# Two score steps of a pair moved together in the step order of both attentions

## The chip, the cores and the metric

The kernel runs on one core of a Trainium2 chip. The metric is the device time of one execution in microseconds (us), the median of several runs. TensorE does matrix products, ScalarE and VectorE work on their results, GpSimd does little here, SyncE issues the loads. Each engine runs its own instructions in program order and waits on semaphores for the others. TensorE writes its products into PSUM, eight banks of 128 x 512 float32 each.

## The reference

A model of three mixers: a first block of two layers over 528 positions (16 learned ones and 512 tokens) and a second block. The first layer's mixer has two attentions side by side, and only these are touched by the change. Both are causal softmax attentions with 8 heads each:

```
s = einsum(q, k) * scale            # plus F[t] - F[s] in the forgetting attention
s = where(mask, s, NEG)
p = softmax(s)
o = einsum(p, v)                    # 64 values a head
```

The forgetting attention has heads of 64 with RMS-normed queries and keys. The latent attention (MLA) has 64 plain and 32 rotated dimensions a head; its queries, keys and values are projected from normed latents of 384 and 256 columns, which makes work between and beside the attentions. After both come the output projection, an MLP, a layer with a short convolution, another MLP and the second block.

## The kernel before

All of float32 matrix work is done with operands split in a high and a low part, three products for one. The eight attention pairs are numbered c = 0 to 7, with two heads in each: c = 0 to 3 are the forgetting attention, c = 4 to 7 the latent one. Pairs are pipelined: while pair c is being finished, the scores of pair c + 1 are prepared. `fox_ring` (L143) writes TensorE's order out as a list of steps, which `fox_pe` runs one after the other:

- `("s", c, i)`, called plain step si here (L739): scores with queries down and keys along, in four query blocks i of 128. They are used for the row maximum alone, which VectorE takes (L924). s3 is 512 keys wide, s2 400, s1 272, s0 256.
- `sm` : the same for the 16 learned positions (maximum at L931, combined at L934).
- `nt`, the turn (L830): VectorE's negated maxima are transposed; VectorE then writes them as rows (L941, L942, "shift").
- `("u", c, j)`, called turned step uj here (L756): scores with keys down and queries along, shifted by the maxima. ScalarE takes their exponentials into `prob` (L872): 128x1024 for u0, 128x832 for u1 (with 16x32 at L871), 128x544 for u2, 128x288 for u3.
- `pm` (L846) and `pv` (L859): the products of probabilities with values, 4 and 20 matrix products. `pv` has banks of its own.
- `lat` (pairs 1 and 2, L1106): sums of squares of the latents. ScalarE makes a scale of them (L1032, L1033), VectorE multiplies the latents by it (L1039). `bq` and `bk` (pairs 4 and 5, L1096): an inverse norm broadcast for the queries and keys of pair c + 2; VectorE multiplies by it (L1188 and L1189 for bq, L1195 and L1196 for bk), ScalarE and VectorE then split the results (L1174 to L1182, L1200 to L1207).

All steps but `pv` and `sum` share three buffers of two PSUM banks each, dealt out in turn: step n takes buffer n % 3. `fox_take` (L688) makes a step wait until the buffer's last user, the step three places before it in the list, has been read:

```
older = [x for x, n in fox_nth.items() if n < fox_nth[step] and fox_slot[x] == fox_slot[step]]
reader = {"s": "max", "sm": "meta_max", "nt": "shift", "u": "exp", "pm": "meta_out"}[kind]
pe.wait_ge(fx[reader], fox_count(*older[-1]))
```

The order of ScalarE and VectorE is written by hand as well, in `fox_act` (L863) and `fox_dve` (L926). ScalarE runs for each pair: exponential of u0, conversion of pair c - 1's output (L889), exponential of u1, then in pair 1

```
latent_scale_act(act, 0)
mla_weights_act(act, 0)
```

(L903, L904: the scale, then conversions of a weight matrix, L1058 and L1060) and in pair 2 the same with another matrix (L1063), then the exponentials of u2 and u3 and, after `pv`, the inverse of the sums (L883 to L886). In pairs 4 and 5 the splitting of a query follows the exponential of u2 and that of a key the one of u3. VectorE runs for each pair: the output (L949, L950), the maximum of s3, the remainder of the output (L954), in pairs 1 and 2 the latent products, in pairs 4 and 5 the products of bq; then the maximum of s2, in pairs 4 and 5 the products of bk; the maximum of s1; in pairs 1 and 2 the remainder of the weights (L1069, L1074), in pairs 4 and 5 that of the rotated query (L1200, L1201); the maximum of s0; the meta maximum; the shift.

Of the kernel before, what the change touches and what calls it, by code (L numbers as in the profile page):

```python
# [142 lines left out]
def fox_ring():  # L143

    out = [("sm", 0), ("s", 1, 3), ("nt", 0), ("s", 1, 2), ("u", 0, 0), ("s", 1, 1), ("u", 0, 1), ("s", 1, 0), ("u", 0, 2), ("sm", 1),
           ("u", 0, 3), ("pm", 0), ("nt", 1), ("pv", 0)]
    for c in range(1, 4):
        body = [("u", c, 0), ("s", c + 1, 3), ("u", c, 1), ("lat", c - 1), ("s", c + 1, 2), ("u", c, 2), ("s", c + 1, 1), ("u", c, 3),
                ("s", c + 1, 0), ("sm", c + 1), ("pm", c), ("nt", c + 1), ("pv", c)]
        out += [x for x in body if x[1] < (2 if x[0] == "lat" else 4)]  # L150
    out += [("pq", 0), ("pq", 1), ("sum", 0), ("pq", 2), ("sum", 1), ("pq", 3), ("sum", 2), ("pr", 0), ("sum", 3), ("pr", 1), ("sum", 4), ("rot", 0),
            ("pr", 2), ("sum", 5), ("rot", 1), ("pr", 3), ("sum", 6), ("rot", 2), ("pk", 0), ("sum", 7), ("rot", 3), ("pk", 1),
            ("sum", 8), ("pk", 2), ("sum", 9), ("pk", 3), ("sum", 10), ("kr", 0), ("kr", 1), ("sum", 11), ("sum", 12), ("bq", 4), ("v", 0),
            ("bk", 4), ("v", 1), ("v", 2), ("bq", 5), ("s", 4, 3), ("s", 4, 2), ("bk", 5), ("s", 4, 1), ("s", 4, 0), ("sm", 4), ("nt", 4)]
    for c in range(4, 8):
        body = [("u", c, 0), ("s", c + 1, 3), ("u", c, 1), ("bq", c + 2), ("s", c + 1, 2), ("u", c, 2), ("bk", c + 2), ("s", c + 1, 1), ("u", c, 3),
                ("s", c + 1, 0), ("sm", c + 1), ("pm", c), ("nt", c + 1), ("pv", c)]
        out += [x for x in body if x[1] < 8]
    return out
# [13 lines left out]
def program(nc, io, out):  # L173

    ctx = ExitStack()
    with ctx:
# [490 lines left out]
        fx = sems("fox", "squares sums full scales normed q_hi q_lo max meta_max shift exp meta_out pv inv o_done out_hi out_lo")  # L667
        fox_first = [[("s", 0, 3), ("s", 0, 2)], [("s", 0, 1), ("s", 0, 0)], []]
        fox_order = fox_ring()
        fox_slot, fox_nth = {}, {}  # L670
        for n, step in enumerate(sum(fox_first, [])):
# [1942 lines left out]
```

## Time and profile before

| | |
|---|---|
| median of 3 runs | 1817.6 us (1816.02 to 1818.84) |
| the profiled execution | 1817.29 us, span 1815.5 us |
| granted TensorE clock, mean of the span | 0.967 |
| TensorE (PE) busy | 1743.3 us, 96% |
| VectorE (DVE) busy | 885.2 us, 49% |
| ScalarE (ACT) busy | 633.8 us, 35% |
| first attention (pairs 0 to 3) | from about 143 to 221.5 us |
| second attention (pairs 4 to 7) | from 285.4 to 364.5 us |

### The profile page before, as it was taken

The page shows a single profiled execution, that of the slowest core. Times are in us where ns is not written, and L with a number is a line of the kernel's source. Part 1 is how long each engine was busy: PE and PEld are TensorE (multiplying, and loading weights), DVE is VectorE, ACT ScalarE, POOL GpSimd, SP SyncE. Part 2 cuts the span into 40 slices and gives each one's busy share as a digit, 9 for nine tenths or more (in the row PEclk, how much of TensorE's full clock was granted, in tenths as well). Part 3 has the DMA queues.
Part 4 walks back from the last instruction along what each step waited for, and adds up shares of the span by engine and source line. Part 5 has one row for each costly group of instructions (what it writes and reads, how often), then busy time and mean ns, then how long its engine had stood idle before and what let it go on. Part 6 is the DMA issues. An engine that isn't in the chain of part 4 may idle for free.

```text
span 1815.5 us, 27268 instructions
## 1 busy us (share of the span) xinstructions
PE 1743.3 (96%) x11417; PEld 1511.6 (83%) x11417; DVE 885.2 (49%) x1193; ACT 633.8 (35%) x980; POOL 142.4 (8%) x151
## 2 busy tenths in 40 slices
PE   7999898989999999999999999999999999889998
PEld 6997566789999999999887888888877886666987
DVE  5533346455343333565566333444566477534362
ACT  4523424423232222321233222323344465641222
POOL 1000000032000000220023000000231000003200
PEclk9999898999999999999999999999999999967999
DMA  5240001022232222222223232322364760001001
GB/s 177 71 96 5 7 1 47 2 71 93 93 93 93 93 83 89 87 89 93 93 93 93 94 99 97 103 94 92 95 88 70 94 94 18 1 11 47 1 24 70
DMA packets 137545, 129.57 MB, mean 71 GB/s; under 512 B 17633, under 2 KB 135512, under 8 KB 137452
## 3 DMA queue, kind: packets, MB, share of 16 engines
q1 hardware_dynamic: 137250, 128.18, 26.0%
q8 instruction: 69, 1.13, 0.3%
q14 instruction: 24, 0.20, 0.0%
q10 hardware_dynamic: 202, 0.06, 0.0%
HBM read 126.14 MB, written 2.10 MB: 71 GB/s over the span
## 4 chain that ended last, share of the span: by engine, by line
PE 91%; DVE 4%; ACT 3%; issue 1%; SPq 1%; DMA 0%; ACTq 0%; DVEq 0%
PE ps L430 71%; PE ps L859 3%; PE ps L756 1%; PE ps L739 1%; PE ps L1865 1%; PE ps L1090 1%; PE ps L2125 1%; PE ps L2135 1%; PE ps L2132 1%; PE ps L1152 1%; PE ps L2152 0%; PE ps L2160 0%; PE ps L764 0%; SPq L2376 0%; PE ps L2083 0%
## 5 line engine op out<-in xcount | busy, mean ns | idle before, releaser
L403 ACT ACTIVATE w_hi<-raw 128x1024 fp32r<-128x1024 f32 (+1 forms) x227 | 239.3, 1055 | 825.8 <-PE ps L430 819.6
L430 PE MATMUL ps<-x_hi,w_hi 128*128 128x258 f32 (+4 forms) x1640 | 450.5, 327 | 3.6 <-DVE x_lo L450 2.8
L430 PE MATMUL ps<-x_lo,w_hi 128*128 128x258 f32 (+4 forms) x1640 | 444.4, 323 | 0.0
L430 PE MATMUL ps<-x_hi,w_lo 128*128 128x258 f32 (+4 forms) x1640 | 443.4, 323 | 0.0
L411 DVE TENSOR_TENSOR w_lo<-raw,w_hi 128x1024 fp32r<-128x1024 f32 (+1 forms) x227 | 294.6, 1299 | 96.8 <-ACT w_hi L403 96.7
L430 PEld LDWEIGHTS ps<-x_hi,w_hi 128*128 128x128 f32 (+2 forms) x1640 | 273.4, 188 | 34.7 <-issue 3.8
L430 PEld LDWEIGHTS ps<-x_lo,w_hi 128*128 128x128 f32 (+2 forms) x1640 | 272.3, 187 | 28.0 <-issue 2.4
L430 PEld LDWEIGHTS ps<-x_hi,w_lo 128*128 128x128 f32 (+2 forms) x1640 | 272.2, 188 | 25.7
L430 PE MATMUL ps<-a_hi,w_hi 128*128 128x258 f32 (+1 forms) x1024 | 281.8, 326 | 10.3 <-issue 10.3
L430 PE MATMUL ps<-a_hi,w_lo 128*128 128x258 f32 (+1 forms) x1024 | 281.6, 326 | 0.0
L430 PE MATMUL ps<-a_lo,w_hi 128*128 128x258 f32 (+1 forms) x1024 | 281.4, 326 | 0.0
L430 PEld LDWEIGHTS ps<-a_hi,w_hi 128*128 128x128 f32 x1024 | 172.3, 190 | 28.5 <-issue 11.2
L430 PEld LDWEIGHTS ps<-a_hi,w_lo 128*128 128x128 f32 x1024 | 172.6, 190 | 17.1
L430 PEld LDWEIGHTS ps<-a_lo,w_hi 128*128 128x128 f32 x1024 | 172.5, 190 | 17.0
L1313 DVE TENSOR_TENSOR h<-h,ps 128x512 f32<-128x512 f32 (+1 forms) x88 | 60.7, 689 | 229.5 <-PE ps L430 229.5
L1380 DVE SCALAR_TENSOR_TENSOR tmp<-ps,scale_bc 128x516 f32<-128x516 f32 (+1 forms) x64 | 44.4, 693 | 172.1 <-PE ps L430 162.2
L460 POOL TENSOR_TENSOR acc<-h 128x516 f32<-128x516 f32 (+1 forms) x4 | 4.2, 1045 | 874.2 <-DVE h L1313 874.2
L463 POOL TENSOR_TENSOR acc<-acc,sq 128x516 f32<-128x516 f32 (+1 forms) x28 | 59.8, 2136 | 2.2
L450 DVE SCALAR_TENSOR_TENSOR x_lo<-h,vec,x_hi 128x516 fp32r<-128x516 f32 (+2 forms) x40 | 58.1, 1466 | 0.1
L859 PE MATMUL ps<-prob,v_one 128*128 128x512 f32 (+4 forms) x160 | 49.9, 455 | 4.4 <-ACT prob L872 4.4
L859 PEld LDWEIGHTS ps<-prob,v_one 128*128 128x128 f32 (+1 forms) x160 | 30.5, 207 | 23.7 <-issue 11.5
L2240 POOL TENSOR_TENSOR gdn_LB<-gdn_LT,gdn_masks 128x128 f32<-128x128 f32 x56 | 24.3, 473 | 291.8 <-DVE gdn_LT L2261 262.4
(397 smaller groups left out, 1868.7 us busy)
## 6 DMA issues: line engine op xcount, KB each, us to landing
raw<-in_w_mlp_up SPq DMA_DIRECT2D x32, 1024.0 KB, 5.4
raw<-in_w_mlp_down SPq DMA_DIRECT2D x32, 1024.0 KB, 4.9
raw<-in_w_in SPq DMA_DIRECT2D x16, 1024.0 KB, 9.1
raw<-in_w_in_conv SPq DMA_DIRECT2D x12, 1024.0 KB, 5.1
raw<-in_w_in_attn SPq DMA_DIRECT2D x8, 1024.0 KB, 5.2
raw<-in_w_out_attn SPq DMA_DIRECT2D x4, 1024.0 KB, 5.0
raw<-in_w_out_conv SPq DMA_DIRECT2D x4, 1024.0 KB, 5.0
raw<-in_w_out SPq DMA_DIRECT2D x4, 1024.0 KB, 5.2
```

Of the source, the lines that this page charges most:

```text
L403: act.activation(dst, panel_view(p)[:, :, o:o + w], ACT.Copy).then_inc(w_hi_ok, 1)
L411: dve.tensor_tensor(lo, panel_view(p)[:, :, o:o + w], hi.bitcast(F32), ALU.subtract).then_inc(w_lo_ok, 1)
L430: ins = pe.matmul(pair_of_banks[t % 2][0:m, b, 0:c], w[:, k, :], x[:, k, x0:x0 + c], start=(k == order[0] and n == 0), stop=(k == order[-1 ...
L450: dve.scalar_tensor_tensor(x_lo[:, c, f:], h[:, c, f:], col(*nm.gain(c)), x_hi[:, c, f:].bitcast(F32), ALU.mult, ALU.subtract).then_inc(x_ ...
L463: pool.tensor_tensor(acc[:, f:], acc[:, f:], sq[:, f:], ALU.add).then_inc(acc_ok, 1)
L739: ins = pe.matmul(slot[0:nq, x, c0:c0 + nk], q, k, start=(n == 0), stop=(n == last))
L756: ins = pe.matmul(slot[0:nk, x, c0:c0 + nq], k, q, start=(n == 0), stop=(n == last))
L859: ins = pe.matmul(ps[:, 6 + x, 512 - n:512], v_one[0:rows, j, c % 4, 64 * x:64 * x + P], prob[0:rows, x, p0:p0 + n], start=(j == 0), stop= ...
L1090: ins = pe.matmul(slot[:, bank, 0:wd], a, b[:, x0:x0 + wd], start=(k == 0 and n == 0), stop=(k == len(w) - 1 and n == 2))
L1313: dve.tensor_tensor(like(dst, width), like(dst, width), in_psum(pair_of_banks[t % 2], width), ALU.add).then_inc(evicted, 1)
L1380: dve.scalar_tensor_tensor(like(tmp[:, j % 2, 0:w], w), in_psum(pair_of_banks[(t0 + j) % 2], w), 0.0, like(scale_bc[:, f:], w), ALU.max, A ...
L2240: ins = pool.tensor_tensor(blk(LB, h, j), blk(LT, h, j), gmask[:, 1 + i, :], ALU.mult)
```

## The change

In `fox_ring`, the list of TensorE's steps for the pairs 1 to 7 is reordered. The second turned step u1 moves ahead of plain step s3 of the next pair, and so stands right behind u0. The later turned steps stand earlier too, each ahead of the `lat`, `bq` or `bk` step or of a plain step, and s2 and s1 of the next pair now follow each other behind them. The number of steps, their buffers' rotation and each step's content are the same; the step three places before each is another one. The steps of pair 0, the part between the attentions, and the orders of the other engines are not touched.

```
     for c in range(1, 4):
-        body = [("u", c, 0), ("s", c + 1, 3), ("u", c, 1), ("lat", c - 1), ("s", c + 1, 2), ("u", c, 2), ("s", c + 1, 1), ("u", c, 3),
+        body = [("u", c, 0), ("u", c, 1), ("s", c + 1, 3), ("u", c, 2), ("lat", c - 1), ("u", c, 3), ("s", c + 1, 2), ("s", c + 1, 1),
                 ("s", c + 1, 0), ("sm", c + 1), ("pm", c), ("nt", c + 1), ("pv", c)]
...
     for c in range(4, 8):
-        body = [("u", c, 0), ("s", c + 1, 3), ("u", c, 1), ("bq", c + 2), ("s", c + 1, 2), ("u", c, 2), ("bk", c + 2), ("s", c + 1, 1), ("u", c, 3),
+        body = [("u", c, 0), ("u", c, 1), ("s", c + 1, 3), ("u", c, 2), ("bq", c + 2), ("u", c, 3), ("bk", c + 2), ("s", c + 1, 2), ("s", c + 1, 1),
                 ("s", c + 1, 0), ("sm", c + 1), ("pm", c), ("nt", c + 1), ("pv", c)]
```

## Rows read from the trace of the kernel before

**Rows 1.** The page, chain that ended last, share of the span by engine.
```profile
PE 91%; DVE 4%; ACT 3%; issue 1%; SPq 1%; DMA 0%; ACTq 0%; DVEq 0%
```
**Rows 2.** TensorE's waits, 160 to 222: total us, times, longest.
```profile
PE ps L756 <- DVE shift_cols L924: 3.4, 2, 2.1
```
**Rows 3.** Timeline, TensorE, pair 1: start, us, work, [idle before].
```profile
164.24 2.94 PE L1106 MATMUL ps<-mla_sq,t_ones 128*128 128x264 f32 x12
...
167.10 0.45 PE L739 MATMUL ps<-fox_hi 64*128 64x400 f32 x2
...
167.85 0.44 PE L739 MATMUL ps<-f_rows,sel_r 64*128 64x400 f32 x2
...
171.71 0.39 PE L756 MATMUL ps<-fox_hi 64*128 64x256 f32 x2 [2.06 <-DVE shift_cols L924]
...
174.79 0.45 PE L830 MATMUL ps<-t_ident,shift_cols 128*128 128x128 f32 x1
```
**Rows 4.** Timeline, ScalarE, pair 1.
```profile
164.89 0.84 ACT L872 ACTIVATE prob<-ps 128x832 f32<-128x832 f32 x1
167.21 0.70 ACT L1032 ACTIVATE mla_sq<-ps,t_zeros 128x528 f32<-128x528 f32 x1 [1.48 <-PE ps L1106]
...
168.50 1.47 ACT L1058 ACTIVATE uq_hi<-uq 128x1536 fp32r<-128x1536 f32 x1
...
171.43 0.60 ACT L872 ACTIVATE prob<-ps 128x544 f32<-128x544 f32 x1
```
**Rows 5.** Timeline, VectorE, pair 1.
```profile
168.62 2.13 DVE L1039 SCALAR_TENSOR_TENSOR lat<-lat,vec,mla_sq 128x528 f32<-128x528 f32 x3 [2.40 <-ACT mla_sq L1033]
170.67 1.62 DVE L924 TENSOR_REDUCE shift_cols<-ps 128x2 f32<-128x800 f32 x2
...
173.87 0.45 DVE L924 TENSOR_REDUCE shift_cols<-ps 128x2 f32<-128x288 f32 x1
```
**Rows 6.** Timeline, ScalarE and VectorE, pair 2.
```profile
186.70 0.84 ACT L872 ACTIVATE prob<-ps 128x832 f32<-128x832 f32 x1
...
189.41 1.90 ACT L1063 ACTIVATE ukv_hi<-ukv 128x2048 fp32r<-128x2048 f32 x1
...
190.91 1.61 DVE L924 TENSOR_REDUCE shift_cols<-ps 128x2 f32<-128x800 f32 x2
```
**Rows 7.** Timeline, VectorE, pair 5.
```profile
320.98 1.23 DVE L924 TENSOR_REDUCE small<-ps 128x2 f32<-128x1024 f32 x1
...
322.85 0.76 DVE L1188 SCALAR_TENSOR_TENSOR z<-z,vec,ps 128x528 f32<-128x528 f32 x1
...
324.14 0.98 DVE L924 TENSOR_REDUCE shift_cols<-ps 128x2 f32<-128x800 f32 x1
325.04 0.75 DVE L1195 SCALAR_TENSOR_TENSOR z<-z,vec,ps 128x528 f32<-128x528 f32 x1
...
328.20 0.45 DVE L924 TENSOR_REDUCE shift_cols<-ps 128x2 f32<-128x288 f32 x1
```
**Rows 8.** Timeline, TensorE, pair 5: step bq, and the turn.
```profile
322.21 0.28 PE L1096 MATMUL ps<-rn_r,each_r 64*128 64x264 f32 x1
...
329.58 0.30 PE L830 MATMUL ps<-t_ident,shift_cols 128*128 128x128 f32 x1
```
**Rows 9.** Value products of pairs 1, 3, 4; busy time by stretch, with granted clock.
```profile
175.03 7.02 PE L859 MATMUL ps<-prob,v_one 128*128 128x512 f32 x20
...
213.23 8.36 PE L859 MATMUL ps<-prob,v_one 128*128 128x512 f32 x20 [4.40 <-ACT prob L872]
...
311.42 5.53 PE L859 MATMUL ps<-prob,v_one 128*128 128x512 f32 x20
...
175.10:178.50 3.40, 3.40 (x7) 1.67 (x7) 0.83 (x2) 0.00 (x0) 0.00 (x0) 0.55 0.03 5
...
208.20:213.20 5.00, 0.62 (x4) 0.52 (x4) 3.18 (x5) 4.94 (x10) 0.00 (x0) 0.56 0.00 0
```
**Rows 10.** Busy time, pair 6: stretch, us, PE, PEld, DVE, ACT, POOL, clock, DMA, GB/s.
```profile
338.00:352.00 14.00, 13.94 (x167) 11.29 (x163) 6.54 (x12) 3.27 (x7) 0.00 (x0) 1.00 0.01 2
```

More of the change, by code:

```diff
@@ L147, in fox_ring @@
     for c in range(1, 4):
-        body = [("u", c, 0), ("s", c + 1, 3), ("u", c, 1), ("lat", c - 1), ("s", c + 1, 2), ("u", c, 2), ("s", c + 1, 1), ("u", c, 3),
+        body = [("u", c, 0), ("u", c, 1), ("s", c + 1, 3), ("u", c, 2), ("lat", c - 1), ("u", c, 3), ("s", c + 1, 2), ("s", c + 1, 1),
                 ("s", c + 1, 0), ("sm", c + 1), ("pm", c), ("nt", c + 1), ("pv", c)]
@@ L155, in fox_ring @@
     for c in range(4, 8):
-        body = [("u", c, 0), ("s", c + 1, 3), ("u", c, 1), ("bq", c + 2), ("s", c + 1, 2), ("u", c, 2), ("bk", c + 2), ("s", c + 1, 1), ("u", c, 3),
+        body = [("u", c, 0), ("u", c, 1), ("s", c + 1, 3), ("u", c, 2), ("bq", c + 2), ("u", c, 3), ("bk", c + 2), ("s", c + 1, 2), ("s", c + 1, 1),
                 ("s", c + 1, 0), ("sm", c + 1), ("pm", c), ("nt", c + 1), ("pv", c)]
```

## The prediction

> **What bounds the kernel now.** I read the chain of waits first: 91% of it is TensorE [rows 1]. So a new order of TensorE's steps is worth what it does to the times at which TensorE stands still, and to the clock after them; the matrix work itself is the same in both kernels. Then I read the list of waits and the timeline of the two attentions pair by pair, TensorE, ScalarE and VectorE each by itself. The reader is to see three things there. First, TensorE stands still for 3.4 us in two places, waiting for a maximum of L924 [rows 2]. The longer is in pair 1, 2.06 us ahead of the fourth turned step (u3) at 171.71 [rows 3]: that step takes the buffer of plain step s2, and its maximum (170.67) had to queue on VectorE behind the three latent products of L1039 [rows 5]. The other is the same place in pair 2. Second, the clock falls behind such a stall: the granted clock is 0.55 of full between 175.1 and 178.5, and the 20 value products of pair 1 take 7.02 us where those of pair 4 take 5.53 [rows 9]. Third, in pair 6, without latent or rope work, TensorE is busy for 13.94 of 14.00 us [rows 10]: there is nothing to win in it.
>
> **What the change does.** No instruction is added or taken away, on any engine. ScalarE and VectorE keep their order; only TensorE's is changed, and with it who hands a score buffer to whom, since each step takes the buffer of the step three places ahead of it and waits for its reader. Pairs 3 and 7 have no scores of a next pair, so their list stays the same, and pair 6 has the new order but no extra step. There remain pairs 1, 2, 4 and 5.
>
> *Pair 1.* The first three steps are now u0, u1, s3. They take as long as u0, s3, u1 and end at 164.24, where the latent step starts before [rows 3]; u2 follows there. The latent step took u0's buffer and now takes u1's. The exponential of u1 runs on ScalarE at 164.89 for 0.84 us [rows 4] and can't be earlier, because the conversion of pair 0's output stands ahead of it; it ends at 165.73. With 0.06 us until TensorE moves (my reading of such hand-overs), the latent step starts at 165.79 instead of 164.24, after a stall of some 0.9 us. It has 2.97 us from its start to ScalarE's next instruction (167.21 - 164.24) [rows 3, 4], the latent scale, now at 168.76. u3 no longer waits (the maximum of s3 is done by 165.8), so the old stall is gone.
>
> What is late next is s2. It stands three places behind u2 and so needs the exponential of u2. On ScalarE this comes after the latent scale (168.50 - 167.21 = 1.29 us) and the weight conversions (171.43 - 168.50 = 2.93 us) [rows 4], whose order isn't changed: 168.76 + 1.29 + 2.93 = 172.98, and 0.60 us for the exponential itself = 173.58; s2 starts at 173.64. TensorE has finished u3 near 169.4, so it stands still for about 4.2 us. Before, only s0 needed that exponential, and it came in time. Behind s2 on TensorE stand s1, s0, the meta steps and the turn (nt), and VectorE waits with them: maximum of s2, of s1, the weight remainder, maximum of s0, the meta maximum. This VectorE chain sets the turn: it comes 0.92 us after the maximum of s0 begins (174.79 - 173.87) [rows 3, 5]. So the pair is late by as much as the maximum of s2 is late. s2's last product ends 1.19 us after its start (167.85 + 0.44 - 167.10) [rows 3], and 0.03 us later VectorE starts: 174.86 instead of 170.67. Pair 1: +4.2 us.
>
> *Pair 2*, by the same steps [rows 6]: exponential of u1 done at 186.70 + 0.84 = 187.54, latent step at 187.60; it has 8 products instead of 12, 2.94 x 8/12 = 1.96 us, and 0.03: 189.59; scale 1.29: 190.88; the one conversion 1.90: 192.78; exponential 0.60 and 0.06: s2 at 193.44; its maximum 1.22 later at 194.66 instead of 190.91. Pair 2: +3.8 us.
>
> *Pair 5.* Here the two extra steps are broadcasts (bq and bk) read by VectorE's products. s2 now needs bq's reader, and s0 bk's reader, which VectorE runs only after the maximum of s2. u0, u1, s3 end at 322.21, as u0, s3, u1 do before [rows 8]; the last product of s3 ends 0.16 us later and its maximum starts at 322.40. From there VectorE's chain by distances between starts [rows 7]: maximum of s3 and output remainder 322.85 - 320.98 = 1.87, bq's products 324.14 - 322.85 = 1.29, so s2 starts at 322.40 + 3.16 + 0.04 = 325.60 (TensorE is free at about 325.0). Its maximum starts 1.25 us later, 326.85, and takes 0.90; bk's products, the maximum of s1 and the rope remainder take 328.20 - 325.04 = 3.16: 330.91, and 0.92 on the turn: 331.83 instead of 329.58 [rows 8]. Pair 5: +2.25 us. *Pair 4* has no output remainder (L954), 0.6 us less on VectorE, of which TensorE's own work takes 0.2 back: +1.85 us.
>
> Pair 6 stays at nothing: u3 needs the exponential of u1, s2 the maximum of s3, s1 the exponential of u2, and TensorE's own work covers each of them by some tenths of a us; without that cover I put it at under 0.5 us. Waits together: 4.2 + 3.8 + 2.25 + 1.85 = 12.1 us.
>
> **The clock.** The trace has no stall of 4.2 us in pairs 1 and 2, so its price is bounded by rows. The old stall cost 7.02 - 5.53 = 1.49 us in the value products behind it; pair 3, with a stall of 4.40 us, takes 8.36 us for the same products, a cost of 2.83 [rows 9]. Lower bound: the new stalls cost nothing, because the slow stretch falls where TensorE waits anyway, and the old ones give back 1.49 us each in two pairs, -3.0. Upper bound: twice the cost of pair 3, less the old 1.49, in both (2 x 4.2), and 1.5 us in each of pairs 4 and 5: +11.4. I take pair 3's row for pairs 1 and 2, as its stall is nearest in length: 2.83 - 1.49 = 1.34, a little of it beside VectorE's chain, so +1.2 each; and one stretch of 1.5 us for pairs 4 and 5 together, whose stalls of some 1.2 us are about as long as the smaller of the two old ones. Clock: +3.9 us.
>
> The Trainium skill (TensorE: Matmul & The Clock Gate, Terms) puts the penalty at the throttled time multiplied by one minus the granted share, whatever the engine does in it. In pair 3 the clock is at 0.56 for the 5.0 us from 208.2 on, of which TensorE works 0.62 us [rows 9]. The page's rule would count 5.0 x 0.44 = 2.2 us there on top of the 2.83 of the products; with that in pairs 1 and 2 the estimate would be 1837.7. The row shows nearly no work that could be slowed, so I leave it out.
>
> **Sum.** The profiled execution took 1817.29 us (span 1815.5), 0.3 below the median of 1817.6, so nothing is to be corrected. 1817.3 + 12.1 + 3.9 = 1833.3 us.
>
> **Rivals.**
> *A, faster: the removed wait is not replaced.* Its place is ScalarE's exponential of u2 in pairs 1 and 2. If it ran ahead of the latent scale and the conversion, s2 would start at once, the 3.4 us of stalls would go and with them 3.0 us of slow clock: 1817.3 - 6.4 = 1810.9. For it: the stall ahead of u3 is real and the change does take it away. Against: the exponential stands at 171.43, behind the conversion [rows 4]. It decides if s2 starts before about 170. 5%.
> *B, half the price: VectorE's chain in pairs 4 and 5 is hidden*, because bq and bk leave VectorE their input earlier or run beside a neighbouring step. Then only pairs 1 and 2 pay: 1817.3 + 8.0 + 2.4 = 1827.7. Against: maximum of s2, bk's products and s0 are one serial chain. 12%.
> *C, the clock pays its upper bound*: 1817.3 + 12.1 + 11.4 = 1840.8. For it: several stalls now stand close together. Against: TensorE's busy time between them. 10%.
> *D, the change does not do what it says*: the pairs' late ends are caught up in waits that pair 3 has anyway, 1817. Against: pair 3's stall comes from ScalarE's work behind its own u1, and so moves along. 3%.
>
> **How the numbers follow.** Forecast 70%, A 5, B 12, C 10, D 3. The range of 1826 to 1840 holds the forecast and B and reaches nearly to C. A measurement of this kernel can tell about 0.2% (3.6 us) from no change; B, C and the forecast are all slower by more: slower 0.91, same 0.04, faster 0.05.
>
> **What would show it.** In the changed profile: in pair 1 a stall of about 4 us ahead of a plain step with 400 columns, released by ScalarE's exponential of 128x544; the latent step 1.5 us later, behind the exponential of 128x832; no stall ahead of the fourth turned step; in pairs 4 and 5 stalls of about 1 us ahead of the 256-column plain step, released by the rope product L1196; pairs 3, 6 and 7 as before. The prediction is wrong if s2 runs right behind u3 in pairs 1 and 2, or if the time moves outside these attentions.

## The result and the profile after

The changed kernel takes 1831.95 us (median of 4, 1830.38 to 1837.56), the one before 1817.56 us; the ratio is 1.0085 with a 95% interval of 1.0062 to 1.0108. That is 14.4 us more, where 15.7 were forecast over the median.

The page of the changed kernel, busy line and shares of the chain. TensorE's busy time grows by 7.3 us with the same 11417 products, which is the first sign of a slower clock:

```profile
PE 1750.6 (96%) x11417; PEld 1517.3 (83%) x11417; DVE 885.7 (48%) x1193; ACT 633.5 (35%) x980; POOL 142.0 (8%) x151
...
PE 91%; ACT 4%; DVE 3%; issue 1%; SPq 1%; DMA 0%; ACTq 0%; DVEq 0%
```

TensorE's waits in pairs 1 to 3 of the changed kernel (total us, times, longest), which answer to [rows 2]. The 3.4 us for the maximum are gone from L756; 7.0 us for an exponential stand at L739, the plain steps, and 1.6 us at the latent step L1106. The 4.4 us at L859 and the 1.2 us at L846 are pair 3's, as before.

```profile
PE ps L739 <- ACT prob L872: 7.0, 2, 4.0
PE ps L859 <- ACT prob L872: 4.4, 1, 4.4
PE ps L1106 <- ACT prob L872: 1.6, 2, 0.8
PE ps L846 <- ACT prob L872: 1.2, 1, 1.2
```

Pair 1 of the changed kernel, TensorE: the latent step, u3, the first product of s2, the turn and the value products; compare [rows 3, 9]. Pair 1 begins (u0) at 158.72 here and at 160.17 before, so 1.45 is to be added to compare times.

```profile
164.33 2.94 PE L1106 MATMUL ps<-mla_sq,t_ones 128*128 128x264 f32 x12 [0.79 <-ACT prob L872]
167.20 0.39 PE L756 MATMUL ps<-fox_hi 64*128 64x256 f32 x2
...
172.18 0.70 PE L739 MATMUL ps<-fox_hi 64*128 64x400 f32 x2 [4.05 <-ACT prob L872]
...
179.04 0.45 PE L830 MATMUL ps<-t_ident,shift_cols 128*128 128x128 f32 x1
179.29 7.91 PE L859 MATMUL ps<-prob,v_one 128*128 128x512 f32 x20
```

The same pair, ScalarE [rows 4]. The reader is to see the exponential of u2 (with u3's, x2) behind the conversions of L1058 and L1060; s2 starts 0.66 us after it begins.

```profile
163.44 0.84 ACT L872 ACTIVATE prob<-ps 128x832 f32<-128x832 f32 x1
167.31 0.70 ACT L1032 ACTIVATE mla_sq<-ps,t_zeros 128x528 f32<-128x528 f32 x1 [3.03 <-PE ps L1106]
...
168.59 1.47 ACT L1058 ACTIVATE uq_hi<-uq 128x1536 fp32r<-128x1536 f32 x1
169.96 1.65 ACT L1060 ACTIVATE uq_rope_hi<-uq 128x512 fp32r<-128x512 f32 x3
171.52 0.90 ACT L872 ACTIVATE prob<-ps 128x544 f32<-128x544 f32 x2
```

And VectorE [rows 5]: the latent products are done by 170.8, and then it stands still for 3.42 us, waiting for s2.

```profile
168.72 2.12 DVE L1039 SCALAR_TENSOR_TENSOR lat<-lat,vec,mla_sq 128x528 f32<-128x528 f32 x3 [3.86 <-ACT mla_sq L1033]
174.27 0.99 DVE L924 TENSOR_REDUCE shift_cols<-ps 128x2 f32<-128x800 f32 x1 [3.42 <-PE ps L739]
```

The clock, from the busy time by stretch of the changed kernel (columns as in rows 10): pair 1, pair 2, then in pair 1 the stall, the work right behind it, the first value products, and the whole stretch at the lower level. The granted clock is 0.76 and 0.75 over the pairs, 0.50 in the work behind the stall. The slow stretch begins near 170.7, still inside the stall, and lasts until about 184.

```profile
158.72:187.12 28.40, 23.57 (x170) 17.64 (x169) 10.63 (x17) 9.86 (x18) 0.00 (x0) 0.76 0.01 1
187.12:214.05 26.93, 23.14 (x167) 17.16 (x167) 10.39 (x16) 8.73 (x15) 1.68 (x3) 0.75 0.04 11
168.10:172.10 4.00, 0.03 (x2) 0.00 (x0) 2.12 (x3) 4.00 (x7) 0.00 (x0) 0.82 0.00 0
172.10:175.30 3.20, 3.12 (x26) 2.68 (x28) 0.99 (x1) 0.32 (x2) 0.00 (x0) 0.50 0.00 0
179.30:183.70 4.40, 4.40 (x9) 2.35 (x8) 0.83 (x2) 0.12 (x1) 0.00 (x0) 0.50 0.01 4
...
170.70:184.50 13.80, 12.32 (x70) 9.53 (x71) 5.12 (x9) 1.90 (x5) 0.00 (x0) 0.51 0.00 1
```

Pair 5 of the changed kernel, VectorE and TensorE [rows 7, 8]: s2 waits for bq's products, s0 for bk's, and those for the maximum of s2.

```profile
334.29 1.23 DVE L924 TENSOR_REDUCE small<-ps 128x2 f32<-128x1024 f32 x1 [1.45 <-PE ps L739]
...
336.16 0.76 DVE L1188 SCALAR_TENSOR_TENSOR z<-z,vec,ps 128x528 f32<-128x528 f32 x1
...
339.00 0.99 DVE L924 TENSOR_REDUCE shift_cols<-ps 128x2 f32<-128x800 f32 x1 [1.46 <-PE ps L739]
339.90 0.76 DVE L1195 SCALAR_TENSOR_TENSOR z<-z,vec,ps 128x528 f32<-128x528 f32 x1
```

```profile
337.59 0.45 PE L739 MATMUL ps<-fox_hi 64*128 64x400 f32 x2 [0.62 <-DVE rope_q L1189]
...
341.33 0.39 PE L739 MATMUL ps<-fox_hi 64*128 64x256 f32 x2 [1.15 <-DVE rope_k L1196]
...
344.03 0.30 PE L830 MATMUL ps<-t_ident,shift_cols 128*128 128x128 f32 x1
```

From u0 to u0 (or to the next stage) the traces give, in us:

| kernel | pair 1 | pair 2 | pair 3 | pair 4 | pair 5 | pair 6 |
|---|---|---|---|---|---|---|
| before | 21.81 | 20.62 | 18.92 | 19.95 | 18.30 | 17.24 |
| changed | 28.40 | 26.93 | 18.09 | 21.83 | 20.85 | 17.25 |
| e1, new order in pairs 1 to 3 | 28.38 | 26.91 | 18.09 | 19.67 | 18.30 | 17.24 |
| e2, new order in pairs 4 to 7 | 23.12 | 20.89 | 17.62 | 24.77 | 20.84 | 17.24 |
| e3, exponential of u2 first | 24.35 | 22.02 | 18.83 | 25.03 | 20.86 | 17.28 |
| e4, bk before the maximum | 27.24 | 25.67 | 18.08 | 20.81 | 19.84 | 17.26 |
| e5, TensorE busy in the stall | 26.03 | 24.62 | 17.65 | 24.78 | 20.83 | 17.24 |
| e6, old order, work moved | 17.85 | 16.96 | 13.51 | 19.65 | 18.29 | 17.25 |
| e7, new order, work moved | 20.11 | 19.22 | 11.90 | 21.84 | 20.84 | 17.25 |

The 13.1 us between the spans of the two profiled executions are +6.6, +6.3, -0.8, +1.9 and +2.6 in pairs 1 to 5 (16.5), and -3.5 us outside: -1.45 before pair 1, -0.6 between the attentions, -1.4 behind them. Nothing was changed there, and the same stretches differ by as much between executions of kernels that are equal in them: over these nine traces the part ahead of pair 1 ends between 158.66 and 160.17, the part between the attentions takes 74.2 to 75.4 us, and the part from the start of pair 7 on 1461.7 to 1465.3.

The pairs themselves vary too, so a row of this table is one execution, not a mean. e2 has the old order in pairs 1 to 3, and they differ from before by +1.3, +0.3 and -1.3 us. e4 has the changed kernel's instructions and orders in pairs 1 and 2, and they are 1.16 and 1.26 us shorter. The -0.8 us in pair 3 is no effect of the new order: its steps are the same in both, and e2, with the old order ahead of it, has the still shorter 17.62.

### The profile page after: what moved, and what is told of

Same layout as the page of the kernel before. It is cut to its first block, busy times and chain, and to the rows that moved or that the text cites. A ratio compares the mean times of both kernels' runs of the same rounds, so it can differ in the third digit from the quotient of the medians.

```text
span 1828.6 us, 27268 instructions
## 1 busy us (share of the span) xinstructions
PE 1750.6 (96%) x11417; PEld 1517.3 (83%) x11417; DVE 885.7 (48%) x1193; ACT 633.5 (35%) x980; POOL 142.0 (8%) x151
## 4 chain that ended last, share of the span: by engine, by line
PE 91%; ACT 4%; DVE 3%; issue 1%; SPq 1%; DMA 0%; ACTq 0%; DVEq 0%
PE ps L430 70%; PE ps L859 3%; PE ps L739 2%; PE ps L756 1%; PE ps L1865 1%; PE ps L1090 1%; PE ps L2125 1%; PE ps L2135 1%; PE ps L2132 1%; PE ps L1152 1%; PE ps L764 1%; PE ps L2152 0%; PE ps L2160 0%; PE ps L2083 0%; PE ps L2085 0%
## 5 line engine op out<-in xcount | busy, mean ns | idle before, releaser
L859 PE MATMUL ps<-prob,v_one 128*128 128x512 f32 (+4 forms) x160 | 51.4, 466 | 4.4 <-ACT prob L872 4.4
L859 PEld LDWEIGHTS ps<-prob,v_one 128*128 128x128 f32 (+1 forms) x160 | 31.5, 213 | 24.2 <-issue 11.9
```

The lines of the kernel that those rows point to most:

```text
L859: ins = pe.matmul(ps[:, 6 + x, 512 - n:512], v_one[0:rows, j, c % 4, 64 * x:64 * x + P], prob[0:rows, x, p0:p0 + n], start=(j == 0), stop= ...
```

## The experiments

The theory: in pairs 1 and 2 the new order makes s2 wait for ScalarE's exponential of u2, which stands behind background work; in pairs 4 and 5 it makes s2 and s0 waits in a serial chain with VectorE; the clock falls behind the longer stalls. The rivals are those of the prediction: B, that the half in pairs 4 and 5 is hidden; C, that the clock is most of the price; and that the releaser shown in the profile is only the last one in time. Seven kernels were run, each timed against the kernel before.

**e1 and e2, one half each.** Each has one of the two changed lines of `fox_ring`.

```
e1:  for c in range(1, 4):  new body        for c in range(4, 8):  old body
e2:  for c in range(1, 4):  old body        for c in range(4, 8):  new body
```

> The new order in the forgetting attention alone (pairs 1 to 3), the old one in pairs 4 to 7. Theory (s2 of pairs 1 and 2 waits for ScalarE's exponential of u2 behind the latent scale and the weight conversion, and the clock falls behind the stall): pairs 1 and 2 are longer by 6.6 and 6.3 us as in the changed kernel's trace, less what moves elsewhere: +10 to +12 us over before, 1828 to 1830. Rival B of the prediction turned round (the price lies half in pairs 4 and 5): under +8 us. If two costs are not additive, this and the next run don't sum to the +14 of the whole change.

> The new order in the latent attention alone (pairs 4 to 7). Theory (serial chain of VectorE: products of bq, maximum of s2, products of bk, then s0): +1.85 in pair 4 and +2.25 in pair 5, nothing in pairs 6 and 7, no slow clock in addition: +4.1 us, 1821.7. If the stalls of 1.2 us bring a slow stretch: +5.6. Rival B (the chain is hidden): +0 to +1.

e1: 1824.42 us, ratio 1.0043 (1.0029 to 1.0056), +8.0 us over the 1816.44 of the kernel before in this comparison. e2: 1822.33 us, ratio 1.0041 (1.0027 to 1.0055), +5.9 us. The sum, 13.9, is near the 14.4 of the whole change; each half is known to some 2.5 us. Rival B is out by e2, which costs 5.9 where B said 0 to 1. The same rival turned round, that half of the price lies in pairs 4 and 5, is not: e1 came out below its 10 to 12 us, right at the 8 that was its bound to that rival, and the intervals of the two halves overlap.

e1's trace is of the slowest of its five executions (1827.1 us), and in it pairs 1 and 2 are as long as in the changed kernel to 0.02 us. e4's trace shows that they can be shorter with the same work: the stalls ahead of s2 are the same (4.06 and 2.92 us against 4.05 and 2.92), but the mean clock of the pairs is 0.81 and 0.80 instead of 0.76 and 0.75.

```profile
158.82:186.06 27.24, 22.39 (x170) 16.91 (x169) 10.63 (x17) 9.86 (x18) 0.00 (x0) 0.81 0.00 1
186.06:211.73 25.67, 21.86 (x167) 16.15 (x166) 10.30 (x16) 8.73 (x15) 1.68 (x3) 0.80 0.04 11
```

e2 is nearer to the +5.6 with a slow stretch, and its trace shows one. Pair 4 takes 24.77 us there and 21.83 in the changed kernel, with the same stall ahead of s0 (1.16 and 1.14 us). The stretch behind that stall, e2 first, then the changed kernel:

```profile
309.60:314.70 5.10, 5.07 (x44) 3.83 (x45) 4.42 (x10) 2.52 (x5) 0.00 (x0) 0.74 0.00 0
```

```profile
320.40:325.00 4.60, 4.46 (x46) 3.56 (x47) 4.07 (x11) 2.53 (x5) 0.00 (x0) 1.00 0.00 0
```

But only half of the 2.94 us between the two lies there. The other half, 1.43 us, is lost ahead of the stall: s0 starts 14.96 us after u0 in e2 (309.62 - 294.66) and 13.53 in the changed kernel (320.48 - 306.95). Every trace has a slow stretch at the start of pair 4, behind waits of 1.33 and 1.02 us that stand in the old order too, and in e2 it lasts longer. The first 7.04 us of pair 4, e2 first, then the changed kernel:

```profile
294.66:301.70 7.04, 7.04 (x60) 6.06 (x62) 1.87 (x3) 1.02 (x1) 0.00 (x0) 0.52 0.01 2
```

```profile
306.95:313.99 7.04, 7.04 (x76) 5.82 (x78) 1.88 (x3) 1.96 (x3) 0.00 (x0) 0.76 0.00 0
```

So a stall of 1.15 us in pair 4 is followed by a slow stretch in some executions and not in others, and a single trace does not tell the mean.

**e3, the exponential of u2 first.** The changed kernel, one instruction of ScalarE moved in pairs 1 and 2.

```
                 probs(c, 1)
+                if c in (1, 2):
+                    probs(c, 2)
                 if c == 1:
                     latent_scale_act(act, 0)
                     mla_weights_act(act, 0)
...
-                probs(c, 2)
+                if c not in (1, 2):
+                    probs(c, 2)
```

> The changed kernel, with ScalarE's exponential of u2 in pairs 1 and 2 moved ahead of the latent scale and the weight conversion. Theory: the stalls ahead of s2 (4.05 and 2.92 us) go, since nothing else holds s2 back; the next late thing is s0, which needs the exponential of u3, still behind the conversion: a stall of about 2.3 us in pair 1 and 1.2 in pair 2. The turn comes some 2.5 us earlier in each, and 1 us of slow clock less: about 7 us under the changed kernel, +7 over before. Rival (the stall ahead of s2 is the wait for the maximum of s3 or for VectorE's latent products, and the releaser shown is only the last one in time): no change to within 1 us, +14.

1826.67 us, ratio 1.0056 (1.0043 to 1.0070), +10.2 us over before where the changed kernel has +14.4. TensorE of e3, pair 1: s2 follows u3 without a stall, and the next late step is s0, by 2.24 us; ScalarE has the exponential of u3 behind the conversion.

```profile
167.91 0.37 PE L756 MATMUL ps<-shift_rows,f_rows 64*128 64x256 f32 x2
168.11 0.35 PE L739 MATMUL ps<-fox_hi 64*128 64x400 f32 x2
...
172.12 0.39 PE L739 MATMUL ps<-fox_hi 64*128 64x256 f32 x2 [2.24 <-ACT prob L872]
```

```profile
170.12 1.65 ACT L1063 ACTIVATE uq_rope_hi<-uq 128x512 fp32r<-128x512 f32 x3
171.68 0.39 ACT L872 ACTIVATE prob<-ps 128x288 f32<-128x288 f32 x1
```

The stall moves as the theory says, so the releaser in the profile is the cause. Pairs 1 and 2 are 4.05 and 4.91 us shorter than in the changed kernel's trace, 9.0 together, and 6.5 shorter than in e4's; 7 were expected. The median shows less, 4.2 us, and the two intervals overlap a little. In this trace pair 4 is slow as in e2's (25.03 us), which takes 3.2 of it back; that this is so in the other executions is not shown. The Trainium skill (TensorE: Matmul & The Clock Gate, Architectural detail) calls the queues of ScalarE and VectorE strictly first in, first out; the trace agrees: what helped was the place in ScalarE's order alone.

**e4, bk before the maximum.** The changed kernel, VectorE's order in pairs 4 and 5.

```
                 for i in (3, 2, 1, 0):
+                    if c < 6 and i == 2:
+                        mla_k_normed(dve, c - 2)
                     if c < 7:
                         fox_largest_dve(dve, c + 1, i)
...
-                    if c < 6 and i == 2:
-                        mla_k_normed(dve, c - 2)
```

> The changed kernel, with VectorE's products of bk (pairs 4 and 5) moved ahead of the maximum of s2. Theory: the 1.14 and 1.15 us stalls ahead of s0 go, because bk's reader no longer waits for s2; the maximum of s2 is not late, as s2 ends when the products do. About 1.2 us gained in each: 2.4 us under the changed kernel, +12 over before. Rival (VectorE as a whole is too late in these pairs, whatever the order): the stall moves to the meta step or the turn, gain under 0.5 us.

1829.92 us, ratio 1.0076 (1.0062 to 1.0090), +13.5 us over before. Against the +14.4 of the changed kernel the intervals overlap, so the times alone do not settle it; the traces do, in which pairs 4 and 5 are shorter by 1.02 and 1.01 us (2.4 together were expected). TensorE's waits of e4 in pairs 4 and 5 and at their start: the 1.14 and 1.15 us ahead of s0 are gone, 0.46 us appear ahead of each turn. So it is the serial chain. What is left behind it is a wait for the turn.

```profile
PE ps L756 <- DVE shift_rows L942: 1.0, 1, 1.0
PE ps L830 <- DVE shift_cols L934: 0.9, 2, 0.5
PE ps L739 <- DVE rope_q L1189: 0.6, 1, 0.6
```

**e5, TensorE busy in the stall.** The changed kernel with products added ahead of s2 in pairs 1 and 2, into a bank that nobody reads at that time.

```
+            if step in (("s", 2, 2), ("s", 3, 2)):
+                pe.wait_ge(fx["o_done"], c - 1)
+                for _ in range(16 if c == 2 else 11):
+                    pe.matmul(ps[:, 6, 0:512], sel_r[:, 0, 0:P], f_rows[:, 0:512], start=True, stop=True)
             fox_take(pe, *step)
```

> The changed kernel, with 16 matrix products of 512 columns (pair 1) and 11 (pair 2) added ahead of s2, into a bank that nobody reads then: TensorE works in the stall instead of standing still. They add work and no result. Theory (pairs 1 and 2 lose 4.2 and 3.8 us to the wait, and the rest of their loss, with what the old kernel already lost, to the slow clock behind the stall, 3.9 us each): the wait stays, the clock stays full, pairs 1 and 2 are shorter by 3.9 us each, 7 to 8 us under the changed kernel, +6.5 over before. Rival (the slow value products come from something else than the standstill, or the added work pushes s2 back): no gain, or a loss up to 1 us.

1828.45 us, ratio 1.0075 (1.0057 to 1.0093), +12.1 us over before where the changed kernel has +14.4. The gain of 2.3 us is a third of the 7 to 8 expected, and by the times it is not clear of the noise: the intervals overlap. The traces show it, with 27 products (6.8 us of TensorE work) more: pairs 1 and 2 are 2.37 and 2.31 us shorter than in the changed kernel's trace and 1.21 and 1.05 shorter than in e4's. Busy time of e5's pairs 1 and 2: the clock is 0.93, not full.

```profile
158.66:184.69 26.03, 23.66 (x188) 17.49 (x187) 10.44 (x17) 9.87 (x18) 0.00 (x0) 0.93 0.01 1
184.69:209.31 24.62, 21.70 (x177) 15.68 (x176) 10.29 (x16) 8.74 (x15) 1.68 (x3) 0.93 0.03 12
```

What the theory had left out is the turn: with the scores at full clock TensorE gets there before VectorE's chain and stands still again, and the clock falls behind that stall.

```profile
177.48 0.30 PE L834 MATMUL ps<-t_ident,shift_cols 128*128 128x128 f32 x1 [1.43 <-DVE shift_cols L938]
```

This run gives the best measure of the wait by itself. From u0 to the turn, pair 1 takes 177.48 - 158.66 = 18.82 us here and 174.79 - 160.17 = 14.62 before: +4.20. Pair 2 takes 17.34 against 13.58: +3.76. The clock is full up to the turn in both kernels (0.99 in pair 2 before). Pair 1, before and then e5:

```profile
160.17:174.79 14.62, 12.45 (x149) 9.98 (x149) 9.52 (x15) 9.87 (x18) 0.00 (x0) 1.00 0.00 1
```

```profile
158.66:177.48 18.82, 16.45 (x166) 12.98 (x165) 9.61 (x15) 9.87 (x18) 0.00 (x0) 1.00 0.00 1
```

The rest of the changed kernel's loss, 6.59 - 4.20 = 2.4 and 6.31 - 3.76 = 2.55 us, is the clock's in that execution. In e4's trace, with the same waits, the rest is 1.2 and 1.3 us.

**e6 and e7, the background work moved.** Both have the same moves, e6 with the old order of TensorE, e7 with the new one. ScalarE does the conversions after the meta output and VectorE the latent products and the weight remainder after the shift, where both wait for the value products.

```
 ScalarE:
-                if c == 1: latent_scale_act(act, 0); mla_weights_act(act, 0)
-                if c == 2: latent_scale_act(act, 1); mla_weights_act(act, 1)
-                if c == 3: latent_hi_act(act)
+                if c in (1, 2): latent_scale_act(act, c - 1)
...
                 meta_out(c)
+                if c in (1, 2): mla_weights_act(act, c - 1)
+                if c == 3: latent_hi_act(act)
                 inverse(c)
 VectorE:
-                    if c in (1, 2) and i == 3: latent_normed_dve(dve, c - 1)
-                    if c in (1, 2) and i == 1: mla_weights_dve(dve, c - 1)
                 if c < 3:
                     largest_meta(c + 1)
                     shift(c + 1)
+                if c in (1, 2):
+                    latent_normed_dve(dve, c - 1)
+                    mla_weights_dve(dve, c - 1)
```

> The old order of TensorE. The latent work of ScalarE and VectorE in pairs 1 to 3 is moved into the 5.5 us of the value products, in which both stand still: ScalarE converts the weights, and in pair 3 the latents, after the meta output; VectorE does the latent products and the weight remainder after the shift. Theory (what costs in both kernels is that work, because score steps wait for what stands behind it): the stalls of pair 1 (2.06), 2 (1.36, 0.65) and 3 (1.25, 4.40) go and with them 1.49, 1.34 and 2.83 us of slow clock: -15 us, about 1802.5. Rival (the work is only pushed on: the inverse of the sums or the projections behind pair 3 become late instead): -5 us or less.

> The changed kernel's order with the same moves of ScalarE's and VectorE's latent work. Theory: s2 now waits only for the exponential of u2 behind the latent scale, a stall of about 1.2 us, after one of 0.8 ahead of the latent step, in pairs 1 and 2; pairs 4 and 5 keep their 4.1 us. So +8 us over the run with the old order and the moves, about 1810.5, under before. Rival (the new order is as good once the other engines' work is out of the way): within 2 us of the run with the old order.

e6: 1802.21 us, ratio 0.9924 (0.9912 to 0.9937), 14.1 us under the kernel before, where 15 were expected. It beats both kernels. Its pairs 1 to 3: in pair 1 TensorE is busy for 17.79 of 17.85 us, in pair 2 for 16.90 of 16.96, at full clock. In pair 3 the stall of 4.40 us is down to 0.17, but the one of 1.25 us, which was expected to go as well, stays at 1.23, and the clock is 0.87.

```profile
159.16:177.01 17.85, 17.79 (x172) 13.47 (x171) 10.63 (x17) 10.08 (x18) 0.00 (x0) 1.00 0.01 2
177.01:193.97 16.96, 16.90 (x166) 12.83 (x165) 10.48 (x16) 8.95 (x15) 2.49 (x3) 1.00 0.07 17
193.97:207.48 13.51, 12.11 (x91) 8.15 (x90) 5.49 (x10) 9.51 (x19) 0.54 (x1) 0.87 0.00 1
```

ScalarE of e6, pair 1: the conversions now stand ahead of the inverse, and 2.62 us are still free between them, so they do not delay it.

```profile
171.45 1.48 ACT L1055 ACTIVATE uq_hi<-uq 128x1536 fp32r<-128x1536 f32 x1
172.84 1.66 ACT L1057 ACTIVATE uq_rope_hi<-uq 128x512 fp32r<-128x512 f32 x3
177.11 0.20 ACT L883 ACTIVATE o_inv<-o_meta 64x4 f32<-64x4 f32 x1 [2.62 <-PE ps L859]
```

e7: 1812.71 us (median of 12, 1808.27 to 1817.69), ratio 0.9982 (0.9971 to 0.9993), 10.5 us over e6 where 8 were expected. In its trace the latent step waits 0.79 us and s2 1.12 us in pair 1; pairs 1 and 2 are 2.26 us each over e6, and pairs 4 and 5 keep their 2.2 and 2.55. Pair 3 goes the other way in these two traces, 11.90 against 13.51, because e7's has full clock there (1.00 against 0.87). The trace is of the fastest of the 12 executions and has no slow stretch behind the stall of pair 4; what the slower ones pay for is not shown. The new order is the worse one with the background work out of the way as well.

## Why the prediction was right

The forecast was 1833.3 us, the median is 1831.95; the direction, the cause and the size held. How the sum is split is less sure: forecast were 10.4 us in pairs 1 and 2 and 5.6 in pairs 4 and 5, and the medians of e1 and e2 give 8.0 and 5.9. That the total is off by only 1.4 us is in part luck. By its steps:

- *Pairs 1 and 2, waits of 4.2 and 3.8 us.* e5 measures 4.20 and 3.76. The latent step starts 5.61 us after u0 (5.62 predicted) and s2 13.46 (13.47 predicted). The sum is that good because every term was the distance between two starts on one engine's row, and no step's content changed.
- *Pair 4, 1.85, and pair 5, 2.25.* Measured 1.88 and 2.55. The 0.3 us in pair 5 is a mis-sized term: the maximum of s2 starts 1.41 us after s2 (339.00 - 337.59), not 1.25, and s2 itself starts 0.1 us later than summed. Pair 4 is mis-sized by as much: the 1.88 is so near because pair 4 of the trace of before has a longer slow stretch at its start. Against e1's, which has the old order there and a start like the changed kernel's, it is 21.83 - 19.67 = 2.16. Pair 6 was put at nothing and is at 0.01.
- *The clock, 1.2 each in pairs 1 and 2, and 1.5 in pairs 4 and 5.* This is the loosest term. Pairs 1 and 2 measure 2.4 and 2.55 in the traces of the changed kernel and e1, and 1.2 and 1.3, as forecast, in e4's. Pairs 4 and 5 pay nothing in the changed kernel's trace; e2, e3 and e5 have a slow stretch behind the stall of pair 4. Taking pair 3 as the model missed one thing: there the stall lies right ahead of the value products, while in pair 1 the steps from s2 to the turn lie between. They run at 0.50 too, which in the changed kernel's trace costs 1.5 us (the turn comes 179.04 - 158.72 = 20.32 us after u0, 18.82 in e5). The sum of the two single executions came out near because too little in pairs 1 and 2 stood against -0.8 us in pair 3 and -3.5 us outside, none of which was forecast or is an effect of the change.
- *Rival A* needed s2 to start early; e3 did that and s0 became the late step, so even then the change loses. *Rival B* is refuted by e2, *D* by the result. *Rival C* is not reached: the clock's share in pairs 1 and 2 is 4.95 us of the 12.9 in the changed kernel's trace (2.5 of 10.5 in e4's), more than forecast there but not most of it.

The Trainium skill's rule (TensorE: Matmul & The Clock Gate, Terms) was left out of the sum; the 1837.7 us worked out with it would have been nearly 6 too many. By that rule, an estimate, pair 1 of the changed kernel loses 28.40 x 0.24 = 6.8 us to the clock and e5's 26.03 x 0.07 = 1.8, a difference of 5.0; the two traces differ by 2.4. The trace does not agree with it. Of the 13.8 us at the lower level from 170.70 on, 1.48 lie in the stall (until 172.18), where there was nothing to slow: 0.7 us by the rule. And at full clock e5 stands still for 1.43 us ahead of the turn, waiting for VectorE, time that the changed kernel fills with slower work. These two explain most of the gap.

## What to carry to other kernels

In a rotation of few buffers a step's place decides whose reader it waits for. Before reordering, write down for each step the one three (or however many) places ahead, find its reader in the other engine's order, and count what stands ahead of that reader. If background work on the reading engine is what delays it, move that work into the shadow of a long stretch of the bounding engine (here 5.5 us of value products): that gained 14.1 us where a new order of the bounding engine lost 14.4. Moving the waiting step only changed which step was late.

## What the runs showed of the hardware

- Five traces have the same stall of 1.14 to 1.16 us in pair 4. It is followed by a slow stretch in e2, e3 and e5 and not in the changed kernel or e7; behind the same stall in pair 5 none of the five has one. The three also have a longer slow stretch at the start of pair 4, behind waits that stand in every kernel. Together these make pair 4 24.8 to 25.0 us instead of 21.8, half of it from each.
- With the same stalls ahead of s2, the time that the clock costs in pairs 1 and 2 was 2.4 and 2.55 us in two traces and 1.2 and 1.3 in a third.
- Products with no result, put into a stall, raised the mean clock of pair 1 from 0.76 (0.81 in e4's trace) to 0.93 and made the pair 1.2 to 2.4 us shorter, although they add 4.0 us of TensorE work to it. On the whole kernel the gain is not clear of the noise.
